# A product-key expert layer behind a hybrid block: 48 gathered tokens beside the block of 128 instead of 32, 336 dense instead of 352

## The reference

```python
def peer(h, wq, k1, k2, u, v):
    q = (xt @ wq).reshape(T, 8, 2, 128)
    s1 = einsum("thd,hnd->thn", q[:, :, 0], k1)        # 128 scores per head and half
    s2 = einsum("thd,hnd->thn", q[:, :, 1], k2)
    v1, i1 = top_k(s1, 16)
    v2, i2 = top_k(s2, 16)
    best, flat = top_k(v1[..., None] + v2[..., None, :], 16)
    experts = e1 * 128 + e2                            # 16384 experts
    gates = softmax(best)
    a = einsum("td,thkd->thk", xb, u[eb])              # 128 experts for each token
    act = gb * gelu(a)
    y = einsum("thk,thkd->td", act, v[eb])
x = x + gate2 * peer(h2, ...)
```

## Time and profile before

| | us |
|---|---|
| median of 3 runs (lowest, highest) | 3135.79 (3130.93, 3138.95) |
| the profiled execution's own time | 3137.47 |
| its span, first to last instruction | 3135.7 |
| PE busy / DVE / ACT / POOL | 2998.2 / 2533.5 / 1030.0 / 839.7 |
| mean granted TensorE clock | 0.977 of 2.4 GHz |
| bytes moved | 893.8 MB, mean 285 GB/s |

### The profile page before, as it was taken

How to read it: one execution, slowest core, us unless ns; L and a number is a source line. 1 busy time by engine, 2 the same in 40 slices (tenths; PEclk the granted TensorE clock), 3 DMA queues, 4 the chain that set the end, 5 groups by cost and what they waited for, 6 DMA issues and landing times.

```text
span 3135.7 us, 41987 instructions
## 1 busy us (share of the span) xinstructions
PE 2998.2 (96%) x17373; PEld 2759.4 (88%) x17373; DVE 2533.5 (81%) x3098; ACT 1030.0 (33%) x1081; POOL 839.7 (27%) x380
## 2 busy tenths in 40 slices
PE   5799989989989999999999999989999999999999
PEld 3687765557778899999999999989999999999999
DVE  7986968756673589999988998854989899898985
ACT  4323243341122333333333333323333334333331
POOL 5600000000030013333123333421444444444440
PEclk8999989989999999999999999999999999999999
DMA  9722223347744468888778988987999999999994
GB/s 368 268 94 77 81 85 138 124 168 302 290 159 180 142 228 326 333 333 321 274 266 343 356 346 337 389 330 285 375 395 389 390 392 392 395 386 398 385 399 164
DMA packets 182257, 893.82 MB, mean 285 GB/s; under 512 B 15680, under 2 KB 77248, under 8 KB 85824
## 3 DMA queue, kind: packets, MB, share of 16 engines
q1 hardware_dynamic: 111376, 491.29, 42.4%
q0 software_dynamic: 46080, 335.56, 26.2%
q10 hardware_dynamic: 24624, 64.45, 5.3%
HBM read 836.71 MB, written 54.53 MB: 284 GB/s over the span
## 4 chain that ended last, share of the span: by engine, by line
PE 84%; DVE 10%; DMA 2%; ACT 2%; issue 1%; SPq 0%; ACTq 0%; DVEq 0%; PEldq 0%
PE bank L1909 10%; PE bank L1911 10%; PE bank L1910 10%; PE bank L1968 10%; PE bank L1969 10%; PE bank L1970 10%; PE bank L1606 3%; PE bank L1608 3%; PE bank L1607 3%; DVE ada_w L944 2%; PE bank L1944 2%; PE bank L1843 2%; PE bank L1844 2%; PE bank L1845 2%; DMA ada_w<-wada 1%
## 5 line engine op out<-in xcount | busy, mean ns | idle before, releaser
L475 POOL DMA_INDIRECT u_row<-u_rows,urow_i x128 | 285.6, 2231 | 823.7 <-DVE u_row L1374 559.0
L1909 PE MATMUL bank<-act_hi,w_hi 128*128 128x352 f32 x1376 | 447.7, 325 | 8.0 <-DVE low L906 8.0
L1910 PE MATMUL bank<-act_lo,w_hi 128*128 128x352 f32 x1376 | 445.0, 323 | 0.0
L1968 PE MATMUL bank<-wt_hi,w_hi 128*128 128x352 f32 x1360 | 439.5, 323 | 4.9 <-DVE w_lo L906 4.4
L1969 PE MATMUL bank<-wt_lo,w_hi 128*128 128x352 f32 x1360 | 438.4, 322 | 0.0
L1911 PE MATMUL bank<-act_hi,low 128*128 128x352 f32 x1024 | 332.1, 324 | 0.0
L1911 PE MATMUL bank<-act_hi,w_lo 128*128 128x352 f32 x1024 | 330.3, 323 | 0.0
L1970 PE MATMUL bank<-wt_hi,w_lo 128*128 128x352 f32 x1024 | 330.3, 323 | 0.0
L1970 PE MATMUL bank<-wt_hi,low 128*128 128x352 f32 x1024 | 329.3, 322 | 0.0
L486 POOL DMA_INDIRECT u_row<-v_rows,urow_i x96 | 232.2, 2418 | 271.3 <-DVE y_g L1521 249.5
L1374 DVE SCALAR_TENSOR_TENSOR u_row<-u_row,h2t 128x2048 f32<-128x2048 f32 x128 | 288.9, 2288 | 13.4 <-DMA u_row<-u_rows,urow_i 13.3
(11 more groups left out here) (340 smaller groups left out, 7234.3 us busy)
## 6 DMA issues: line engine op xcount, KB each, us to landing
ada_w<-wada SPq DMA_DIRECT2D x80, 1024.0 KB, 5.5
w_raw<-u SPq DMA_DIRECT2D x64, 1024.0 KB, 5.9
raw<-u SPq DMA_DIRECT2D x64, 1024.0 KB, 5.6
w_raw<-v SPq DMA_DIRECT2D x64, 1024.0 KB, 9.1
raw<-v SPq DMA_DIRECT2D x64, 1024.0 KB, 6.8
w_raw<-win SPq DMA_DIRECT2D x27, 1024.0 KB, 4.9
gelu_scratch<-gelu_s ACTq DMA_DIRECT2D x128, 176.0 KB, 8.4
gate_scratch<-g_chunk ACTq DMA_DIRECT2D x11, 2048.0 KB, 12.2
```

Source lines behind the costliest of these rows:

```text
L475: pool.indirect_dma_start(u_row[n % 3][:], None, urow_d, bass.IndirectOffsetOnAxis(ap=col, axis=0)).then_inc(u_row_loaded[n % 3], 16)
L1909: pe.matmul(out, wh[:, k, :], HD(k), start=(k == 0), stop=False)
L1910: pe.matmul(out, wh[:, k, :], LD(k), start=False, stop=False)
L1968: pe.matmul(o, wh[:, 8 * e + d, :], th, start=begin is not None and e == 0, stop=False)
```

## The change

TD goes from 352 to 336, XT from 32 to 48: 32 tokens as before (XA, 4 shares each) and 16 new ones (XB, 8 shares each), which need 16 more gathers from u and 16 more from v. GC goes from 32 to 28, so a piece of `gate_l` is 448 bytes instead of 512 and there are 12 instead of 11. XU, the number of these tokens' u rows gathered by L475, goes from 16 to 44, so the four left are done at the start of the V stage. Hot jobs are 42 instead of 44. The third gate piece is made by ACT (`gate_hots`, eight scaled copies a job) from `hot_eq`, and PE waits for it. ACT issues the unit loads, unit 0 after job 113. A second transposed copy of the tokens (`h2x_b`) is made on PE and ACT after job 3.

```diff
-TD = 352
+TD = 336
-GC = 32
+GC = 28
+XB = 16
+XA = XT - XB
-XU = 16
+XU = 44
...
 (SP)
-            for g in range(2, NKEY - 6):
+            for g in range(2, NKEY + 128):
                 load_raw(g)
-            for s in range(2):
-                sp.wait_ge(g_stored[s], DMA_LEAD + 16 * ((N_CH + 1 - s) // 2))
-                sp.wait_ge(gelu_stored[s], DMA_LEAD + 16 * 6)
-                sp.wait_ge(hot_used[2 * s + 1], LEAD + N_HOTS // 2)
-            load_unit(0)
...
 (ACT)
+            act.activation(x_rep_b[:], x_keep[:, :, 0:XB].unsqueeze(2).broadcast_to([P, KD, P // XB, XB]), ACT.Copy).then_inc(x_rep_ready, 1)
+            def gate_hots(t):
+                u = t % 2
+                act.wait_ge(hot_eq_ready[u], t // 2 + 1)
+                for n in range(8):
+                    ins = act.activation(hot1[2][:, u, n // 2, :, n % 2], hot_eq[:, u, n // 2, :, n % 2], ACT.Copy,
+                                         scale=gate_r[:, 8 * t + n:8 * t + n + 1])
+                ins.then_inc(hot_gated[u], 1)
+            def load_unit(n):
+                if n:
+                    act.wait_ge(wtl_ready, n)
+                rows = slice(4 * n, 4 * n + 4)
+                act.dma_start(wt[:], gelu_d[:, rows, :]).then_inc(wt_loaded, 16)
+                act.dma_start(gate_l[:], gate_d[:, :, rows, :].rearrange("c p i t -> p c i t")).then_inc(wt_loaded, 16)
+                if u == HOT - 1:
+                    act.wait_ge(tabt_used, 1)
+                    gate_hots(0)
                 if HOT <= u < HOT + N_HOTS:
                     keep_hots(u - HOT)
+                    if u < HOT + N_HOTS - 1:
+                        gate_hots(u - HOT + 1)
-                if u == 119:
+                if u == HOT + N_HOTS + 2:
+                    for s in range(2):
+                        act.wait_ge(g_stored[s], DMA_LEAD + 16 * ((N_CH + 1 - s) // 2))
+                        act.wait_ge(gelu_stored[s], DMA_LEAD + 16 * 6)
+                    load_unit(0)
+                if u == 118:
                     weigh_hi(0)
-                if u == 124:
+                if u == 120:
+                    load_unit(1)
+                if u == 123:
                     weigh_hi(1)
+                if u == 125:
+                    load_unit(2)
...
             for u in range(2):
                 act.wait_ge(gelu_stored[u], DMA_LEAD + 64 * 16)
+            load_unit(3)
...
+                    if r % 4 == 2:
+                        load_unit(4 + 4 * i + r // 4)
...
 (DVE)
-                    for m in range(2 + (3 * h + b) % 2):
+                    for m in range(3 if b else 2):
                         dot(n_dot)
...
+            T_.step(dve.tensor_tensor(parts_b[:], bank[5][:, 0:3 * P].rearrange("p (c q n) -> p c q n", c=3, n=XB),
+                                      eighth[:].unsqueeze(1).unsqueeze(3).broadcast_to([P, 3, P // XB, XB]), ALU.mult))
+            T_.step(dve.reduce_sum(table_b[:], parts_b[:].rearrange("p c q n -> p c n q"), AX_X))
...
-                for j in range(3):
-                    ins = dve.tensor_tensor(hot1[j][:, u], hot1[2][:, u], of_tokens(gate_c[j], tok), ALU.mult)
+                for j in range(2):
+                    ins = dve.tensor_tensor(hot1[j][:, u], hot_eq[:, u], of_tokens(gate_c[j], tok), ALU.mult)
...
-                for m in range(2 if t % 3 == 2 else 1):
-                    dot(n_dot)
+                for m in range(1 if t % 5 == 4 else 2):
+                    if n_dot < P:
+                        dot(n_dot)
+                    else:
+                        dot_x(n_dot - P)
...
             for n in range(HOT + N_HOTS, NKEY):
-                for m in range(2 if n % 2 else 1):
+                for m in range(2 if n % 3 else 1):
...
 (start of V: one dot_x with each of q = 2..5; then v_step only, 24 rows for 16 jobs as before)
-                    row(n)
+                    v_step(n)
...
 (PE)
+            for u in range(2, 4):
+                u_job(u)
+            pe.wait_ge(x_rep_ready, 2)
+            pe.wait_ge(h2x_set, 4)
+            turn_x(x_rep_b)
...
+            for t_i, tab in enumerate((e1_t, e2_t, gate_t)):
+                last = pe.matmul(bank[5][:, t_i * P:(t_i + 1) * P], spread_b[:], tab[:, GB - 1, :], start=True, stop=True)
...
                 pe.wait_ge(hot_ready[u], t // 2 + 1)
+                pe.wait_ge(hot_gated[u], t // 2 + 1)
...
-                            last = pe.matmul(bank[d][:, TD:T - P], y_x[:, cols], sel[:], start=True, stop=True)
+                            pe.matmul(bank[d][:, TD:TD + XB], y_b[:, cols], sel_b[:], start=True, stop=True)
+                            last = pe.matmul(bank[d][:, TD + XB:T - P], y_a[:, cols], sel_a[:], start=True, stop=True)
```

More of the change, by code:

```diff
@@ L216, in build @@
         keys = at("keys", 160, [P, PH_, 2, NKEY])
-        g_chunk = [at(f"g_chunk{s}", 112 + 16 * s, [P, NKEY, GC]) for s in range(2)]
+        g_chunk = [at(f"g_chunk{s}", 112 + 14 * s, [P, NKEY, GC]) for s in range(2)]
         u_row = [at(f"u_row{s}", 164 + 8 * s, [P, D]) for s in range(3)]
@@ L310, in build @@
         hot_ready = [sem(f"hot_ready{s}") for s in range(2)]
+        hot_eq_ready, hot_gated = ([sem(f"{n}{s}") for s in range(2)] for n in ("hot_eq_ready", "hot_gated"))
         hot_used = [sem(f"hot_used{s}") for s in range(4)]
@@ L831, in weigh_hi, with keep_x @@
                 act.activation(wt_hi[n % 4][:], wt[:], ACT.Copy).then_inc(wth_ready, 1)
-            gelu_job(0)
-            gelu_job(1)
-            act.wait_ge(h2x_ready, 4)
-            for j in range(4):
-                act.activation(h2x[:, 4 * j:4 * j + 4, :], bank[4 + j][:].rearrange("p (k t) -> p k t", t=P), ACT.Copy).then_inc(h2x_set, 1)
-            for u in range(2, NKEY):
+            def keep_x(part, to):
+                act.wait_ge(h2x_ready, 4 * part + 4)
+                for j in range(4):
+                    act.activation(to[:, 4 * j:4 * j + 4, :], bank[4 + j][:].rearrange("p (k t) -> p k t", t=P), ACT.Copy).then_inc(h2x_set, 1)
+            for u in range(NKEY):
                 gelu_job(u)
+                if u == 1:
+                    keep_x(0, h2x)
+                if u == 3:
+                    keep_x(1, h2x_b)
                 if u == TAB_G - 2:
@@ L1392, in _ @@
             dve.wait_ge(h2t_set, 4)
+            T_.step(dve.tensor_copy(spread_b[:].rearrange("p (q t) -> p q t", t=XB),
+                                    ident[:, P - XA - XB:P - XA].unsqueeze(1).broadcast_to([P, P // XB, XB])))
             n_dot = 0
@@ L1574, in _ @@
                     else:
-                        row(n + 1)
+                        v_step(n + 1)
                 if i == 0:
-                    dve.memset(y_x[:], 0.0).then_inc(y_x_set, 1)
+                    for y in (y_a, y_b):
+                        dve.memset(y[:], 0.0).then_inc(y_x_set, 1)
             for e in range(10):
@@ L1912, in u_job, with turn_x @@
                 last.then_inc(pe_jobs, 1)
+            def turn_x(rep):
+                for k in range(KD):
+                    last = pe.transpose(bank[4 + k // 4][:, (k % 4) * P:(k % 4 + 1) * P], rep[:, k, :, :].rearrange("p a t -> p (a t)"), ident[:])
+                    if k % 4 == 3:
+                        last.then_inc(h2x_ready, 1)
             for u in range(2):
@@ L1917, in _ @@
             pe.wait_ge(h2t_set, 4)
-            for k in range(KD):
-                last = pe.transpose(bank[4 + k // 4][:, (k % 4) * P:(k % 4 + 1) * P], x_rep[:, k, :, :].rearrange("p a t -> p (a t)"), ident[:])
-                if k % 4 == 3:
-                    last.then_inc(h2x_ready, 1)
-            for u in range(2, TAB + 7):
+            turn_x(x_rep)
+            for u in range(2, 4):
[3 more added lines that the diff above has]
+            turn_x(x_rep_b)
+            for u in range(4, TAB + 7):
                 u_job(u)
```

128 lines of the change are left out of this document (58 added, 70 removed).

## The result

The changed kernel takes 3206.83 us (median of four runs, 3190.19 to 3216.05); the kernel before takes 3137.37 beside it (3130.93 to 3142.16). The ratio is 1.022, 95% interval 1.017 to 1.027: slower by 1.7 to 2.7%, where 3068, a gain, was forecast. The profiled execution took 3200.55, its span is 3198.3, the mean granted clock 0.963 (before: 0.977).

The account below looks back on a forecast made before the run. PE was taken to set the end, with DMA next, then DVE. From the median 3135.8, -80.9 (PE) - 18.1 (unit loads) + 8 + 15 + 4 + 4 = -68 gives 3068, likeliest 3050 to 3085, 8 in 10 3042 to 3112.

Parts of the forecast that it names:

- What PE gains: U and V jobs: matmuls of 336 columns and two fewer hot jobs, less added work, change PE's balance by -80.9.
- The unit loads: Last U jobs: issued earlier by ACT, units 0 and 1 no longer stall DVE and PE; -18.1 booked.
- DMA, jobs 69 to 127: U jobs 69 to 127: DMA work taken as 510 against PE's 495.1; +15 (0 to +32).
- Tables, job 68: Around job 68: PE arrives sooner and DVE has more to do before tile 68's low part; +4 (0 to +7).
- V's own DMA limit: V stage: four jobs take 29.55 by DMA against PE's 29.28, a give-back of 0.27 over 31 periods; +8.
- The start of V: Start of V: tiles and unit 2 meet a fuller queue; +4 (0 to +10).
- 1 (DMA never binds): Whole kernel: DMA never limits, so only the DVE parts come back; 3045, chance 0.14.
- 2 (gate copies): Hot jobs: ACT's gate copies make tile latency PE's clock, 1 a job over 42 jobs; 3110, chance 0.15.
- 3 (448-byte pieces cost more): `gate_l` loads: 448-byte pieces cost more than 512-byte ones; at twice the time each, 3156, slower than before; chance 0.09.
- 4 (unit 0's stall as before): Unit 0: the change is not what it says and the stall stays; 3086, called inside the range; no separate chance.

Follow-up runs that it names:

- a_sp: The changed kernel with the unit loads back on SyncE's queue, units 0 to 2 at about the same jobs: 3135.01 us, ratio to before 1.000.
- b_early: The kernel before with units 0, 1 and 2 two, three and one tiles earlier on SyncE's queue: 3121.10 us, ratio to before 0.996.
- a_half: a_sp with only half of each row fetched from the 67th gathered row of the U jobs on: 3085.65 us, ratio 0.983.
- a_fix: a_sp with hot-job row products spread around the hot-column building, tile 68's low part before the table work, one product behind it: 3117.25 us.
- a_turn: The changed kernel with SyncE waiting, before every fourth tile load in V, until the last unit has landed: 3138.23 us, ratio to before 1.003.
- b_third: The kernel before with only the third gate piece moved from VectorE to ScalarE: 3136.08 us, ratio to before 1.000.
- b_act: The kernel before with only the unit loads moved to ScalarE's queue: 3188.65 us, ratio to before 1.017.

## Why the prediction was wrong, step by step

The time is 139 over the forecast, and by what a_sp shows against what was booked that is about 72 from the unit loads, 40 from the DMA in jobs 69 to 127, 18 from V, 6 from the tables and 4.5 from the end.

- **What PE gains: right.** 7.36 a plain job, 8.81 a hot one. Eight V jobs in the steady part take 59.5 to 59.7 (forecast 59.1).
- **The unit loads: the step that failed.** It booked -18.1. The -18.1 itself is real (b_early: -16), but the step counted ScalarE's time for the issues and the wait for `weigh_lo`, and not what moving to another *queue* does: 0 booked, +72 measured. On SyncE's queue a unit has its turn between tiles (one queue, q1, holds both in the earlier trace rows): in a_sp 1 to 7 tile packets per engine, less than one tile's 8, pass between the first and last piece of a unit of the V loop; on ScalarE's it shares the engines with up to four tiles (32 packets) and with rows, and everything else that ScalarE issues stands behind it. The cover that the step named was ScalarE's idle 4.84 a job; the queue behind the instruction was never looked at. In V a late unit reaches PE through `weigh`, `weigh_hi` and `weigh_lo`. It doesn't make the next one late: from the 22nd on the units take 22.4, 4.7, 11.3, 25.1, 6.0, 28.6, 6.0 and 28.6, as behind a stall the large queues are empty.
- **A rule that wasn't weighed.** By the Trainium skill (DMA: Bandwidth & Descriptors, Queues, rings and completion order) each DMA engine takes the queues that have work in turn, a packet at a time, and a packet is typically some 9 to 17 descriptors. The trace agrees on the turns (201 pieces beside 200 row packets) and not on their length: a turn here is a single piece. By the Trainium skill (the same title, Issuing engines are not separate DMA queues) several issuing engines only save issue time; here the choice of queue is worth 72, so the measurement decides.
- **DMA, jobs 69 to 127: right cause, wrong size.** +15 booked (0 to +32). By a_sp it is 35.1 in the hot jobs and 19.6 in jobs 112 to 127: +55. The sum of bytes was sound (510 against 495 gives 15; a_half's 408 GB/s against 394 gives 13 for the hot jobs alone). What it left out is the rows' time under load: with three row buffers and two products in a job the tightest pairs leave only about 9 us between one product and the next use of its buffer, while the rows that DVE waits for in a_sp are there 10.3 to 16.9 (most 12.5 to 15.5) after POOL begins their issue. Spreading them and the three other steps take 20 of the 55 back. What the other 35 are, bytes (13 in the hot jobs by the estimate) or timing, is in part open; no run had a fourth buffer.
- **Tables, job 68:** +4 booked, +10.3 in a_sp. Before, the low part of tile 68 was ready 0.6 ahead of its use; in a_sp a wait of 4.56 for a row stands in front of it. In a_fix, with the low part taken ahead of the work on the tables and one product behind it, job 68 is at PE's pace.
- **V's own DMA limit:** +8 booked over 31 periods; a_sp gives 26 over pace, a_turn 22. Fourteen times eight jobs at 59.6 (58.6 is the pace) and a share of 1.00 are 15 of it, the disturbed first ones the rest. The start of V: +4 booked, 1 to 4 measured.
- **The rivals.** 1 (DMA never binds) fell: the share is 1.00. 2 (gate copies) fell: b_third costs 0, though with fewer rows on the DMA; and in the hot jobs of the changed kernel and of a_sp PE never waits for a copy of ScalarE's. 3 (448-byte pieces cost more) named the right transfer, and the result is on its side of the range, but for a wrong reason: 25 ns a piece, less than a piece of 512 (27). Its "1.6 times its share of a tile's rate" is a slip; 29 ns against 512 bytes at 2.69 a tile is 1.4 times. By the Trainium skill (DMA: Bandwidth & Descriptors, Specifications) below 512 bytes there is a read-modify-write; no such cost shows here, for loads to SBUF. 4 (unit 0's stall as before) fell: DVE never waits for unit 0. Its 3086 lay just outside the likeliest range that it was said to be inside.
- The end after the last eviction is 2.4 longer than before (4.5 in a_sp), though it has less of the dense work; the cause stays open.

## What to carry to other kernels

A transfer that is moved to another queue changes its company. Ask what it was in turn with, what now runs beside it, and what is issued behind it; many small pieces beside large packets of two busy queues starved here, and the engine that issued next stood for most of the time that they took. When the work is cut down until DMA and compute are level, the average share no longer shows what a late row costs: four steps that left the bytes as they were took 29 us off. The square of four small experiments (part A alone, part B alone, both, none) told what a long argument had not; and the run made for another purpose (a_turn beside a_sp) split the 72 better than the one made for it, whose spread was larger than the effect.

## What the runs showed of the hardware that I had not expected

- Service time of a packet in the records: 9 ns for 4 bytes, 25 for 448, 58 for 1344, 206 for 5376, 309 for 8192, 535 for 14336. That is about 8 ns and 27.2 bytes per ns, with no step at 512.
- The issue of a store on ScalarE took 18.86 us behind 1536 pieces on the same queue (12.14 behind 1408 in b_act), in place of 0.33.
- Queues shared a DMA engine by turns of one packet, whatever its size: 201 of 448 bytes beside 200 of rows in 4 us.
- A wait that was *added* to SyncE (a_turn) made the kernel 69 us faster.
- Behind a stall the granted clock of TensorE was lower for a while: 0.50 in 2947 to 2951, 0.93 over the last third of V, 0.92 over jobs 113 to 127, where before the latter two were 1.00 and 0.95.
